# Two-layer streaming encoder on one core: setup by halves of the tokens, bias tables in eight transfers

## The reference

```python
def rmsnorm(x, g):
    y = xf * lax.rsqrt(jnp.mean(xf * xf, axis=-1, keepdims=True) + EPS)
    return (y * g).astype(x.dtype)

def ffn_half(x, g_pre, g_post, w_gu, w_dn):          # w_gu (1024, 5632), w_dn (2816, 1024)
    return x + 0.5 * rmsnorm(swiglu(rmsnorm(x, g_pre), w_gu, w_dn), g_post)

def trunk_layer(...):
    x = ffn_half(x, g[0], g[1], w_ffn_gu[l, 0], w_ffn_dn[l, 0])
    u = rmsnorm(x, g[2])                              # then six projections u @ w_in
    s = einsum(q, k) * 64 ** -0.5 + bias              # bias = rel_bias[l][:, clip(i - j, -128, 128) + 128]
    ...                                               # band and differential attention, cross-attention
    x = ffn_half(x, g[6], g[7], w_ffn_gu[l, 1], w_ffn_dn[l, 1])
```

## Time and profile before

| | |
|---|---|
| median of 3 runs | 2567.17 us (2567.15 to 2569.9) |
| profiled execution, its own time | 2569.76 us |
| its span | 2568.0 us |
| mean granted TensorE clock | 0.993 |
| PE busy | 2499.1 us (97%), 19325 matmuls |
| DVE, ACT, POOL busy | 1209.4, 911.0, 23.8 us |
| moved by DMA | 229.81 MB, mean 89 GB/s |

### The profile page before, as it was taken

How to read it: one execution, slowest core, us unless ns; L and a number is a source line. 1 busy time by engine, 2 the same in 40 slices (tenths; PEclk the granted TensorE clock), 3 DMA queues, 4 the chain that set the end, 5 groups by cost and what they waited for, 6 DMA issues and landing times.

```text
span 2568.0 us, 47241 instructions
## 1 busy us (share of the span) xinstructions
PE 2499.1 (97%) x19325; PEld 2400.7 (93%) x19325; DVE 1209.4 (47%) x2059; ACT 911.0 (35%) x1650; POOL 23.8 (1%) x55
## 2 busy tenths in 40 slices
PE   7999999999899999999999999999998999999998
PEld 6999999997599899999999999999966989999998
DVE  5444325435747644442364443254467567444324
ACT  4222324224745632222242222242256545222221
POOL 1000000000000000000000000000000000000000
PEclk9999999999999999999999999999999999999999
DMA  6332332433033123233323233333321322232331
GB/s 185 90 90 82 97 91 67 141 100 118 17 95 111 47 85 90 85 96 91 89 67 89 83 90 94 87 108 117 114 71 41 108 67 73 83 90 84 98 89 60
DMA packets 384734, 229.81 MB, mean 89 GB/s; under 512 B 6892, under 2 KB 371454, under 8 KB 384608
## 3 DMA queue, kind: packets, MB, share of 16 engines
q1 hardware_dynamic: 379040, 206.66, 27.2%
q0 software_dynamic: 4368, 16.92, 1.9%
q10 hardware_dynamic: 1200, 4.46, 0.5%
HBM read 214.46 MB, written 18.79 MB: 91 GB/s over the span
## 4 chain that ended last, share of the span: by engine, by line
PE 91%; DVE 5%; ACT 2%; DMA 1%; issue 1%; DVEq 0%; SPq 0%; ACTq 0%
PE psum L675 77%; PE psum L650 4%; PE psum L995 3%; PE psum L733 2%; PE psum L1027 2%; PE psum L688 1%; DVE x L1604 1%; PE psum L1009 1%; DVE u_lo L1555 1%; DMA w_raw<-in_w_ffn_gu 1%; DVE w_lo L1560 0%; ACT w_hi L1210 0%; DVE y_mix L1601 0%; DMA w_raw<-in_w_ckv 0%; DVE y_ffn L1601 0%
## 5 line engine op out<-in xcount | busy, mean ns | idle before, releaser
L675 PE MATMUL psum<-u_hi,w_hi 128*128 128x272 f32 x3840 | 809.3, 290 | 8.6 <-ACT w_hi L1210 3.8
L675 PE MATMUL psum<-u_lo,w_hi 128*128 128x272 f32 x3840 | 804.2, 288 | 0.0
L1210 ACT ACTIVATE w_hi<-w_raw 128x1024 fp32r<-128x1024 f32 (+1 forms) x326 | 365.3, 1122 | 1067.1 <-PE psum L675 1030.8
L675 PEld LDWEIGHTS psum<-u_hi,w_hi 128*128 128x128 f32 x3840 | 607.5, 188 | 12.6 <-ACT w_hi L1210 3.9
L675 PEld LDWEIGHTS psum<-u_lo,w_hi 128*128 128x128 f32 x3840 | 605.3, 188 | 0.0
L1560 DVE TENSOR_TENSOR w_lo<-w_raw,w_hi 128x1024 fp32r<-128x1024 f32 (+1 forms) x326 | 424.2, 1302 | 310.7 <-ACT w_hi L1210 310.6
L675 PE MATMUL psum<-u_hi,w_lo 128*128 128x272 f32 x3840 | 544.3, 289 | 0.0
L675 PEld LDWEIGHTS psum<-u_hi,w_lo 128*128 128x128 f32 x3840 | 506.7, 189 | 0.0
L675 PE MATMUL psum<-h_hi,w_hi 128*128 128x272 f32 x1408 | 301.3, 289 | 0.0
L675 PE MATMUL psum<-h_lo,w_hi 128*128 128x272 f32 x1408 | 300.6, 289 | 0.0
L675 PEld LDWEIGHTS psum<-h_hi,w_hi 128*128 128x128 f32 x1408 | 227.5, 189 | 0.0
(11 more groups left out here) (250 smaller groups left out, 2211.7 us busy)
## 6 DMA issues: line engine op xcount, KB each, us to landing
w_raw<-in_w_ffn_gu SPq DMA_DIRECT2D x176, 512.0 KB, 3.8
w_raw<-in_w_ffn_dn SPq DMA_DIRECT2D x64, 704.0 KB, 4.5
w_raw<-in_w_in SPq DMA_DIRECT2D x48, 512.0 KB, 3.8
w_raw<-in_w_out SPq DMA_DIRECT2D x16, 512.0 KB, 3.7
w_raw<-in_w_ckv SPq DMA_DIRECT2D x16, 512.0 KB, 3.6
bias_tab_dram<-bias_rev_dram POOLq DMA_DIRECT2D x1, 5120.0 KB, 22.5
out<-k_nat POOLq DMA_DIRECT2D x4, 1024.0 KB, 5.0
out<-v_nat POOLq DMA_DIRECT2D x4, 1024.0 KB, 5.8
```

What stands on the lines that cost most here:

```text
L675: pe_last[0] = pe.matmul(psum[:, bank + part, 0:c1 - c0], weight[:, slot, b * 128:(b + 1) * 128], xs[:, c0:c1], start=start, stop=stop)
L1210: return act.activation(out, src, ACT.Copy, scale=scale)
```

## The change

It rewrites the setup in halves and cuts the one table transfer in eight. The computation is the same.

- **Loads.** The tokens of half A come in two pieces of 128 rows (SP, ACT) and a rest of 16 rows, half B in 128 rows (ACT), 112 + 16 rows, and a rest of 16. The two rests share the 32 rows of `x_nat[:, NT]`, whose other rows are cleared by DVE first (`rem_cleared`); both queues wait for that before the rests. The gains are loaded by ACT and SP in place of POOL. SP issues slot 0's first weights behind them, and slot 1's behind one more piece of `x`.
- **PE** turns the gains, then the 8 blocks of half A (three turns a block), then starts the first sweep; three blocks of half B are turned behind the first sweep and five behind the second. The blocks of `x` go round six PSUM banks (`X_BANK`). `setup_vals` is waited for only behind `first_chunks`.
- **DVE** clears, copies the gains, then half A, `cut_lo` of slot 0, half B, `cut_lo` of slot 1, the 16 `low`, and only then the lambda and bias work. **ACT** does seven `high` of half A, then `cut_hi` of slot 0, and so on; the squares follow the `high` of both halves.
- **POOL** stores `bias_rev` and then issues eight transfers of two tables each. Number n (0 to 7) waits until slot 1's load of pair n + 2 has landed. The mask waits for all eight.

```diff
-        for s in range(2):
-            load(0, s, w_gu_v[0][:, :, s * DFF:s * DFF + 128], first=True)
+        sp.dma_start(x_nat[:, 0, :], x_prompt[0, 0:128, :]).then_inc(x_loaded[0], 16)
+        sp.dma_start(gains_nat[16:18, :], mem_norm_g).then_inc(gains_loaded, 16)
+        sp.wait_ge(rem_cleared, 1)
+        sp.dma_start(x_nat[0:16, NT, :], x_prompt[0, 256:H, :]).then_inc(rem_loaded, 16)
+        load(0, 0, w_gu_v[0][:, :, 0:128], first=True)
+        sp.dma_start(x_nat[0:112, 3, :], x_prompt[0, H + 128:SEQ, :]).then_inc(x_loaded[3], 16)
+        load(0, 1, w_gu_v[0][:, :, DFF:DFF + 128], first=True)
...
-        pool.dma_start(tab_dram, bass.AP(rev_dram.tensor, 127, [[768, 16], [-1, 128], [1, TABW]])
-                       ).then_inc(tab_made, 16)
-        pool.wait_ge(tab_made, 16)
+        for t in range(0, 16, 2):
+            pool.wait_ge(w_loaded[1], 16 * (t // 2 + 3))
+            pool.dma_start(tab_dram[t:t + 2], bass.AP(rev_dram.tensor, 768 * t + 127, [[768, 2], [-1, 128], [1, TABW]])
+                           ).then_inc(tab_made, 16)
+        pool.wait_ge(tab_made, 128)
...
+        def turn_x(half, ks):
+            for k in ks:
+                bank, d = X_BANK[half][k], slice(k * 128, k * 128 + 128)
...
+                if half == 0:
+                    turn(psum[:, bank, 0:128], x_nat[:, 0, d])
+                    turn(psum[:, bank, 128:256], x_nat[:, 1, d])
+                    mm = turn(psum[:, bank, 256:384], x_nat[:, NT, d])
...
                 sweep(0, 0, 0, 0)
+                if q == 0:
+                    pe.wait_ge(x_loaded[2], 16)
+                    pe.wait_ge(x_loaded[3], 32)
+                    turn_x(1, range(3))
                 pe.wait_ge(w_lo_ready, 2 * pair + 1)
                 sweep(0, 0, 1, 0)
+                if q == 0:
+                    turn_x(1, range(3, KD))
+                    pe.wait_ge(setup_loaded, 48)
+                    turn(psum[:, 4, KD * 18:KD * 18 + 2], sub_nat[:, :]).then_inc(setup_t, 1)
...
+        act.dma_start(gains_nat[0:16, :], norm_g.rearrange("l i d -> (l i) d")).then_inc(gains_loaded, 16)
+        act.dma_start(x_nat[:, 1, :], x_prompt[0, 128:256, :]).then_inc(x_loaded[1], 16)
+        act.dma_start(x_nat[:, 2, :], x_prompt[0, H:H + 128, :]).then_inc(x_loaded[2], 16)
+        act.dma_start(x_nat[112:128, 3, :], x_sample[0, 0:16, :]).then_inc(x_loaded[3], 16)
+        act.wait_ge(rem_cleared, 1)
+        act.dma_start(x_nat[16:SAMPLE, NT, :], x_sample[0, 16:SAMPLE, :]).then_inc(rem_loaded, 16)
+        act.wait_ge(consts, 2)
+        warm(ACT.Copy)
+        act.wait_ge(layer_gains, 1)
+        for k in range(7):
+            high(0, 0, k, 8)
+        cut_hi(0, 0, first=True)
+        high(0, 0, 7, 8)
+        for k in range(6):
+            high(0, 1, k, 8)
+        cut_hi(0, 1, first=True)
```

More of the change, by code:

```diff
@@ L342, in build @@
     w_hi_ready, w_lo_ready, chunk_done = sem("w_hi_ready"), sem("w_lo_ready"), sem("chunk_done")
-    setup_loaded, x_loaded, consts = sem("setup_loaded"), sem("x_loaded"), sem("consts")
+    setup_loaded, consts = sem("setup_loaded"), sem("consts")
+    gains_loaded, gains_turned, rem_cleared = sem("gains_loaded"), sem("gains_turned"), sem("rem_cleared")
+    x_loaded, rem_loaded, x_first = [sem(f"x_loaded{i}") for i in range(4)], sem("rem_loaded"), sem("x_first")
     iden = sem("iden")
@@ L422, in in_bank @@
         return 6 if (g, m) == (0, 2) else 2 * (m % 2)
+    X_BANK = ((5, 6, 7, 1, 2, 3, 5, 6), (7, 5, 6, 7, 5, 6, 7, 5))
     CQ_BANK = (0, 4, 2, 6)
@@ L1033, in _ @@
         pe.wait_ge(iden, 2)
-        pe.wait_ge(consts, 4)
[L1035 to L1048, removed]
+        pe.wait_ge(gains_loaded, 32)
+        for k in range(KD):
+            mm = turn(psum[:, 4, k * 18:(k + 1) * 18], gains_nat[:, k * 128:(k + 1) * 128])
+        mm.then_inc(gains_turned, 1)
+        pe.wait_ge(x_loaded[0], 16)
+        pe.wait_ge(x_loaded[1], 16)
+        pe.wait_ge(rem_loaded, 32)
+        turn_x(0, range(KD))
+        pe.wait_ge(consts, 4)
         for l in range(DEPTH):
@@ L1261, in high @@
         def high(q, half, k, gain):
-            act.wait_ge(x_ready, 8 * q + (4 * half + k // 2 + 1 if q else k + 1))
+            if q:
+                act.wait_ge(x_ready, 8 * q + 4 * half + k // 2 + 1)
+            else:
+                act.wait_ge((x_first, x_ready)[half], k + 1)
             cols = half_of(half)
@@ L1267, in square_x @@
         def square_x(q, half, p):
-            act.wait_ge(x_ready, 8 * q + (4 * half + p + 1 if q else 2 * p + 2))
+            if q:
+                act.wait_ge(x_ready, 8 * q + 4 * half + p + 1)
+            else:
+                act.wait_ge((x_first, x_ready)[half], 2 * p + 2)
             cols = half_of(half)
@@ L1418, in scale_table @@
             copy(table[:, h % 2, :], dist[:, :], scale=-SLOPES[h]).then_inc(tab_scaled, 1)
[L1421 to L1424, removed]
+        act.dma_start(gains_nat[0:16, :], norm_g.rearrange("l i d -> (l i) d")).then_inc(gains_loaded, 16)
[14 more added lines that the diff above has]
+        cut_hi(0, 1, first=True)
+        for k in range(6, KD):
+            high(0, 1, k, 8)
+        for half in range(2):
+            for p in range(4):
+                square_x(0, half, p)
         act.wait_ge(dist_ready, 1)
@@ L1429, in _ @@
         act.wait_ge(dist_ready, 3)
[L1430 to L1435, removed]
         cut_hi(1, 0)
@@ L1817, in keep_values @@
                               ALU.mult).then_inc(o_kept, 1)
-        for s in range(2):
-            cut_lo(0, s)
+        dve.memset(x_nat[:, NT, :], 0.0).then_inc(rem_cleared, 1)
+        dve.wait_ge(gains_turned, 1)
+        dve.tensor_copy(gains_all[:, :, :], psum[:, 4, 0:KD * 18].rearrange("p (k n) -> p k n", k=KD)).then_inc(setup_vals, 1)
+        dve.wait_ge(setup_vals, 1)
+        dve.tensor_copy(gains[:, :, 8:9], gains_all[:, :, 0:1]).then_inc(layer_gains, 1)
+        for k in range(KD):
+            dve.wait_ge(x_turned, k + 1)
+            dve.tensor_copy(x[:, k, 0:H], psum[:, X_BANK[0][k], 0:H]).then_inc(x_first, 1)
+        cut_lo(0, 0)
+        for k in range(KD):
+            dve.wait_ge(x_turned, KD + k + 1)
+            dve.tensor_copy(x[:, k, H:T], psum[:, X_BANK[1][k], 0:H]).then_inc(x_ready, 1)
+        cut_lo(0, 1)
+        dve.wait_ge(layer_gains, 1)
+        for half in range(2):
+            for k in range(KD):
+                low(0, half, k, 8)
         dve.memset(headsq[:, :], 1.0).then_inc(setup_done, 1)
-        dve.wait_ge(setup_loaded, 80)
-        dve.tensor_copy(bias_rev[:, 511:767], bias_in[:, 256:0:-1]).then_inc(rev_ready, 1)
-        dve.tensor_copy(bias_rev[:, 0:511], bias_in[:, 256:257].broadcast_to([16, 511])).then_inc(rev_ready, 1)
+        dve.wait_ge(setup_loaded, 48)
         for n in range(2 * DEPTH):
```

34 lines of the change are left out of this document (19 added, 15 removed).

## The result

| | before | after |
|---|---|---|
| median | 2568.53 us (2567.15 to 2570.36, 4 runs) | 2599.66 us (2596.9 to 2600.77, 4 runs) |
| profiled execution, its own time | 2569.76 us | 2596.9 us |
| its span | 2568.0 us | 2595.0 us |
| mean granted TensorE clock | 0.993 | 0.986 |

The kernel became 1.2% slower: ratio 1.0118, 95% interval [1.0105, 1.0131], or 31 us between medians. The two profiled executions are 27.1 us apart; the forecast's sum was made against such an execution and gave 23.6.

The account below looks back on a forecast made before the run. PE was taken to bound the kernel, busy 97% of the span. Setup -4.4 and loop stalls +28 gave +23.6 us on the profiled 2569.8, 2593.4, less 2.6 for the median: 2591 us, 0.9% slower; 8-in-10 range 2561 to 2606.

Parts of the forecast that it names:

- Two engines: Table transfers: outermost source count 2 puts each on two DMA engines, 64 long packets each; forecast's chance 0.56.
- rival 1: Table transfers: all 16 engines carry each table, 2.3 us a transfer; only the setup counts, 2563 us; chance 0.27.
- The closed loop: Feed-forward loop: a delayed slot 1 load's landing issues the next table, which delays the next load; 4.5 us stall a table.
- L' = L + 16.6: Slot 1 loads: with one landing at L, the next lands at L', 16.6 us later, against 12.1 of PE.
- the signs: What would show the forecast right, among others eight gaps in PE's row between 85 and 180 us.
- Its first packet comes 1.65 us later: Table transfer: its first packet follows 1.65 us after POOL issues it at the landing of a slot 1 load.
- the table has moved 10 packets by then: When the next slot 1 load starts (L + 3.6), 10 packets are through; the other 54 alternate with the load's, 12.0 us.
- 6 x 4.5 + 0.4: Loop loss: tables 2 to 7 pay 4.5 us each, table 1 pays 0.4; about 28 us lost.
- it costs nothing: Clock falling between PE's waits: at most 1.7 us a pair, 12.1 + 1.7 still under 16.6, so no cost.
- Setup, 4.4: Setup: pair 1 starts at 39.5 instead of 43.9 us, gain 4.4 us, between 0 and 7.
- T0: Setup: time when half A's last rest has landed, taken as 9 us (8 to 13.7); pair 1 starts at T0 + 30.5.
- I let the turns of half B do nothing for the clock: Setup on PE: turns don't raise the clock, so 16 slow matmuls at 0.247 us are charged again behind them.

Follow-up runs that it names:

- strips: The change with each of the eight transfers carrying 16 rows of all sixteen tables (outermost count 16) instead of two whole tables: 2559.38 us, ratio 0.9967.
- The run with every second load: The change with its two-table transfers issued behind every second slot 1 load instead of every one: 2561.44 us, ratio 0.9968.
- Moving the last piece forward: The sixteen-row strips with ACT's queue issuing half A's 16-row rest ahead of half B's two pieces: 2556.34 us, ratio 0.9952.
- the strips with short turns: The sixteen-row strips with the turn of the rests taking 32 rows and a 32 x 32 identity instead of all 128: 2567.44 us, ratio 0.9995.
- With four tables: The change with four transfers of four tables, behind the slot 1 loads of pairs 2, 4, 6 and 8: 2561.02 us, ratio 0.9974.
- the change with one transfer: The change with one transfer of all sixteen tables, started behind pair 2's slot 1 load: 2565.28 us, ratio 0.9993.

## Why the prediction was right, and where not

The sign and the cause were right. The size came out right in part by luck: two terms of the sum were too small, the gain of the setup by 4.7 us and the loss of the loop by 9, and they point in opposite directions.

**Two engines: right.** The choice rested on the deal of the 16 tables in the trace of before. Shown by a DMA share of 0.13 while such a transfer runs, by 2, 4 and 16 outermost entries that land in 16.9, 17.4 and 22.5 us, and by strips of the same bytes in 4.1. The rule that the Trainium skill gives (DMA: Bandwidth & Descriptors, Why a DMA increments its semaphore by 16 and not by 1) agrees, and the exception it notes for direct copies from GpSimd did not apply: rival 1 asked for 2.3 us a transfer. How a count of 1, or one that doesn't divide 16, is dealt, no run here shows; sixteen transfers of one table each gave no result.

**The closed loop: right, with its pacing.** The forecast had L' = L + 16.6 and the stall only because the next table hangs on L'. The run with every second load shows that the stall goes when every other load is left alone; that it is the loop and not the rate is argued, as said there. Of PE's seven waits one came in part, as forecast, and six in full, where the signs spoke of eight.

**Size of a pair, 16.6: too small by 0.9 to 1.0.** "Its first packet comes 1.65 us later" and "the table has moved 10 packets by then" failed. The DMA view of 83 to 84 us (DMA share and GB/s in 40 slices, packets by size):

```profile
GB/s 3 4 4 210 211 5 5 5 6 6 5 5 4 3 207 4 4 4 4 3 4 209 4 4 4 3 4 5 4 209 4 209 5 6 5 5 4 209 4 209
DMA packets 555, 0.05 MB, mean 45 GB/s; under 512 B 547, under 2 KB 547, under 8 KB 555
```

The peaks of about 210 GB/s are the long packets: they start at 83.08, 2.1 us behind the landing of the load before (80.95). The next load's packets come from 84.5 on, where the forecast had them. Until then each of the two engines had moved six of the table's, at 0.25 us each. And the 96 to 98 us:

```profile
GB/s 113 0 10 102 10 102 0 113 10 102 0 10 102 113 0 10 102 10 102 0 113 10 102 0 10 102 113 0 10 102 10 20 31 41 41 41 41 41 41 51
```

The last stands in slice 30 of 40, so they end at 97.5. So 64 packets take 14.4 us. The 58 behind 84.5 take 13.0, 0.224 each, which is the 0.195 + 0.027 of the forecast, but for 58 and not for 54. With 1.1 to landing and cut: 2.1 + 14.4 + 1.1 = 17.6. The forecast's own sum, 6 x 4.5 + 0.4, is 27.4 and not 28. Eight tables at 1.0 more each make it 35.4, and the clock behind the last gap, which "it costs nothing" left out, 37.1 against the 36.8 measured.

**Setup, 4.4: too small by 4.7.** Two steps failed. T0 was 10.96 and not 9: the nineteen rows an engine had more packets of other queues between them than the kernel before showed. In 8 to 10 us queue 10, with ACT's rows of `x`, had 18.1% of the engines and queue 1, SP's, 51.3%, where the earlier trace rows had 77.5% and 12.6%. Moving the last piece forward gave 3.1 back. And "I let the turns of half B do nothing for the clock" was wrong by far more: pair 1 starts at T0 + 23.8, not T0 + 30.5. The sixteen slow matmuls did not come, and the 24 turns of half B took 0.13 instead of 0.26 us. Where the turns did leave the clock low (the strips with short turns), pair 1 started at T0 + 31.05 (11.57 to 42.62), so the rest of this working holds to 0.6 us. I had read thirty turns at 0.26 and a slow sweep as a property of turns; it belonged to the 32-row ones among them. The diff showed that the change made all turns of `x` 128 x 128, and I did not weigh it. The Trainium skill's rule (TensorE: Matmul & The Clock Gate, Part 4: PE-mode transpose), that turns don't count as activity, is contradicted here for 128 x 128 turns; the runs with 32-row turns look as if it held.

**Medians.** The forecast took 2.6 us off the profiled execution. This time the profiled one was the fastest, and the others lie 2.7 to 3.9 us above. That is why 27 us between profiles are 31 between medians.

## What to carry to other kernels

Before a transfer is cut into pieces, look at the outermost count of each piece: it can fix how many engines carry it, and a transfer on few engines delays every load that needs all of them. Cut along a level that leaves the outermost count at 16. Don't let a transfer's issue hang on the landing of a load that this very transfer delays, unless an undisturbed load stands between. And where TensorE starts with turns, try all of them with the full 128 rows: here that started pair 1 by 2.5 to 7.5 us earlier.

## What the hardware showed beyond expectation

- **Short turns keep the clock at 1.2 GHz.** One 32-row turn in three (strips with short turns) or in five (before) was enough for 7.5 us and for 2.5 to 2.9 us in the start of pair 1, each shown by two kernels that differ in this and in what it needs (the other rows cleared first, in the kernel before).
- **The other engines get packets too.** In 40 to 220 us queue 0 carried 8400 packets in the change and 1232 in the strips, for the same tables. The 7168 more are 896 a transfer, 14 x 64: as many as the two busy engines have long ones, for each of the 14 others. With four tables it was 4240, or 752 more a transfer, close to 12 x 64. In the 83 to 84 us above 547 of 555 packets are under 512 B, all of queue 0, and it took 40.7% of 16 engines, where two could give 12.5%. Whether they are what makes the first long packet late was not isolated.
- **The clock also dips behind short waits.** Gaps of PE of 1.7 to 3.8 us were followed by 0.76 to 0.80 in the next 7 or 8 us. Runs of one kernel differ with their mean clock: the change with one transfer took 2560.63 us at a mean of 0.995 and 2570.91 at 0.990.
